# Banded attention heads in tiles of 64 queries of two heads by 128 keys, a quarter of the tokens for four heads in each turn

## The reference

```python
def swa_sink_attention(q, k, v, sinks):      # q: [B,S,8,64], k, v: [B,S,2,64]
    ...
    kb, vb = band(kc), band(vc)              # keys: the chunk before and the own one, 128 in all
    s = jnp.einsum('bnqhgd,bnkhd->bnhgqk', qc, kb).astype(jnp.float32) * scale
    s = s - slopes[None, None, :, :, None, None] * dist[None, :, None, None, :, :]
    s = jnp.where((k_pos >= 0)[None, :, None, None, None, :], s, NEG)
    ...
    m = jnp.maximum(jnp.max(s, axis=-1, keepdims=True), sink)
    p = jnp.exp(s - m)
    denom = jnp.sum(p, axis=-1, keepdims=True) + jnp.exp(sink - m)
    out = jnp.einsum('bnhgqk,bnkhd->bnqhgd', (p / denom).astype(v.dtype), vb)

def forgetting_attention(q, k, v, f_logit):  # 8 heads, block of 128 queries against all keys
    ...
    s = s + c_i[..., None] - c_keys[:, :, None, :]
    s = jnp.where(k_pos[None, :] <= q_pos[:, None], s, NEG)
    p = jax.nn.softmax(s, axis=-1).astype(v.dtype)
```

## Time and profile before

| | |
|---|---|
| median of 3 runs | 2611.76 us (2611.57 to 2616.79) |
| the profiled execution | 2613.85 us, span of its instructions 2612.2 us |
| TensorE busy, matmuls | 2429.0 us (93%), 11856 |
| TensorE weight loads busy | 2010.5 us (77%) |
| DVE busy | 1412.0 us (54%) |
| ScalarE busy | 1189.6 us (46%) |
| DMA packets | 196858, 436.30 MB |

### The profile page before, as it was taken

How to read it: one execution, slowest core, us unless ns; L and a number is a source line. 1 busy time by engine, 2 the same in 40 slices (tenths; PEclk the granted TensorE clock), 3 DMA queues, 4 the chain that set the end, 5 groups by cost and what they waited for, 6 DMA issues and landing times.

```text
span 2612.2 us, 35075 instructions
## 1 busy us (share of the span) xinstructions
PE 2429.0 (93%) x11856; PEld 2010.5 (77%) x11856; DVE 1412.0 (54%) x2376; ACT 1189.6 (46%) x2257; POOL 759.7 (29%) x623
## 2 busy tenths in 40 slices
PE   7999999599999999599889999899999999999978
PEld 6788887488888888388668887688888788888856
DVE  6311111388888788456574446744456665444464
ACT  6211111487888788322255555455553233233232
POOL 2000000011111111123355666765653532100471
PEclk9999999699999999799999999899999999999999
DMA  5333333866766664677545443465447865454563
GB/s 170 121 120 120 121 121 129 192 155 162 175 169 150 160 155 114 172 226 233 176 150 162 148 148 119 133 202 157 142 147 289 298 208 177 146 173 153 206 245 137
DMA packets 196858, 436.30 MB, mean 167 GB/s; under 512 B 19432, under 2 KB 81640, under 8 KB 183144
## 3 DMA queue, kind: packets, MB, share of 16 engines
q1 hardware_dynamic: 190576, 417.86, 51.3%
q0 software_dynamic: 6144, 16.79, 2.7%
HBM read 298.06 MB, written 136.51 MB: 166 GB/s over the span
## 4 chain that ended last, share of the span: by engine, by line
PE 41%; DVE 4%; POOL 3%; DMA 1%; issue 1%; ACT 0%; SPq 0%; ACTq 0%; DVEq 0%
PE f_ps L1901 21%; PE f_ps L1922 19%; POOL h_raw L1618 2%; DVE f_hop_lo L1804 2%; DVE f_op_lo L1793 1%; DMA h_raw<-in_w_down 1%; POOL f_b_late L1618 1%; DVE f_acc L1835 0%; DVE f_op_lo L1796 0%; DMA f_b_late<-in_w_down 0%; DVE f_u L1823 0%; DVE hop_lo L1809 0%; DVE hop_lo L1815 0%; ACT f_hop_hi L1702 0%; DVE f_hop_lo L1815 0%
## 5 line engine op out<-in xcount | busy, mean ns | idle before, releaser
L1901 PE MATMUL f_ps<-f_hop_hi,f_op_hi 128*128 128x512 f32 x768 | 305.3, 398 | 26.6 <-DVE f_u L1823 16.1
L650 POOL DMA_DIRECT2D o_main<-a_o x64 | 40.6, 635 | 926.8 <-ACT a_o L970 820.5
L1901 PE MATMUL f_ps<-f_hop_lo,f_op_hi 128*128 128x512 f32 x768 | 303.9, 396 | 0.0
L1901 PE MATMUL f_ps<-f_hop_hi,f_op_lo 128*128 128x512 f32 x768 | 303.9, 396 | 0.0
L1793 DVE TENSOR_TENSOR f_op_lo<-wu_raw,f_op_hi 128x512 fp32r<-128x512 f32 x160 | 167.1, 1046 | 222.7 <-ACT f_op_hi L1669 222.7
L874 DVE TENSOR_TENSOR a_pt_lo<-a_ps_t,a_pt_hi 128x512 fp32r<-128x512 f32 (+3 forms) x384 | 234.7, 618 | 95.2 <-ACT a_pt_hi L963 92.7
L1796 DVE TENSOR_TENSOR f_op_lo<-h_raw,f_op_hi 128x512 fp32r<-128x512 f32 x224 | 188.5, 844 | 163.9 <-ACT f_op_hi L1673 163.9
L1922 PE MATMUL f_ps<-f_hop_hi,f_op_hi 128*128 128x512 f32 x672 | 262.8, 391 | 12.4 <-DVE f_op_lo L1796 12.4
L1922 PE MATMUL f_ps<-f_hop_lo,f_op_hi 128*128 128x512 f32 x672 | 261.6, 389 | 0.0
L1922 PE MATMUL f_ps<-f_hop_hi,f_op_lo 128*128 128x512 f32 x672 | 261.5, 389 | 0.0
L963 ACT ACTIVATE a_pt_hi<-a_ps_t 128x512 fp32r<-128x512 f32 (+3 forms) x384 | 204.1, 541 | 108.1 <-PE a_ps_t L763 62.7
(11 more groups left out here) (173 smaller groups left out, 5644.9 us busy)
## 6 DMA issues: line engine op xcount, KB each, us to landing
h_raw<-u_ops SPq DMA_DIRECT2D x224, 256.0 KB, 3.8
wu_raw<-in_w_up SPq DMA_DIRECT2D x32, 1024.0 KB, 7.1
u_ops<-f_u SPq DMA_DIRECT2D x128, 256.0 KB, 4.8
u_ops<-f_us SPq DMA_DIRECT2D x96, 256.0 KB, 2.0
proj_hi<-p_o_hi SPq DMA_DIRECT2D x18, 1024.0 KB, 4.0
proj_lo<-p_o_lo SPq DMA_DIRECT2D x18, 1024.0 KB, 6.7
h_raw<-in_w_down SPq DMA_DIRECT2D x32, 512.0 KB, 4.2
h_raw<-in_w_down SPq DMA_DIRECT2D x49, 256.0 KB, 4.1
```

The source lines that it names most:

```text
L1901: last = nc.tensor.matmul(bank[:], w[:, k], h[i][:, k], start=(UP_OPENS[i] and k == 0 and m == 0), stop=(k == 3 and m == 2), skip_group_ch ...
```

## The change

- **Tiles.** A band tile is now 64 queries of two heads (128 rows) by 128 keys, exactly the band of one chunk of 64. Each turn works on a quarter of the tokens (`SPAN` = 512) for the four heads that share a key/value head, not on all tokens for one head. A turn has 16 such tiles as before, in five chunks of 4, 4, 4, 2 and 2 tiles, and 4 band steps instead of 8: 44 steps in all. Each band step is an output block of its own. There are 8 value tiles, in two groups.
- **Order.** Fox block 0's chunks move from steps 0 to 2 of their turn to steps 36 to 41 of the turn before. Block 1's stand at 0 to 4 (before 2 to 7), block 2's at 5 to 11 (8 to 14), block 3's at 12 to 23 (16 to 27), the next band chunks at 26 to 30 (30 to 37). Counted in fox steps, blocks 2 and 3 stay where they were within a step.
- **Loads.** The band loads of a turn become 19 DMAs instead of 10, with half the bytes: queries 64 x 8 x 64 in pieces of 256 bytes, keys and values 64 x 576. `proj_hi` and `proj_lo` get 64 columns of zeros in front. The fox loads keep sizes and number, but go in another order. The band's reciprocals are stored by four DMAs instead of one.

```diff
+PAD = CHUNK
...
+            for dst in (proj_hi, proj_lo):
+                for row in (P + SWA_HEADS * HEAD_DIM, P + (SWA_HEADS + SWA_KV_HEADS) * HEAD_DIM):
+                    sp.dma_start(dst[row:row + P, 0:PAD], zeros[:]).then_inc(pad_stored, 16)
...
-    steps = [("swa", j) for j in range(QT // 2)] + [("fox", b, k) for b in range(QB) for k in range(4 * b + 4)]
+    QUARTERS = SWA_HEADS // SWA_KV_HEADS
+    WINDOWS = S // CHUNK // QUARTERS
+    SPAN = WINDOWS * CHUNK
+    NSW = WINDOWS // 2
+    steps = [("swa", j) for j in range(NSW)] + [("fox", b, k) for b in range(QB) for k in range(4 * b + 4)]
...
-    swa_chunks = [("swa", j) for j in range(QT // 2)]
+    swa_chunks = [("swa", n) for n in range(5)]
+    swa_tiles = [range(0, 4), range(4, 8), range(8, 12), range(12, 14), range(14, 16)]
     chunk_at = [[] for _ in range(NSTEP)]
-    for b, (start, span) in enumerate(((0, 3), (2, 6), (8, 7), (16, 12))):
+    for b, (start, span) in ((1, (0, 5)), (2, (5, 7)), (3, (12, 12))):
         for n, c in enumerate(fox_chunks[b]):
             chunk_at[start + n * span // len(fox_chunks[b])].append(c)
     for n, c in enumerate(swa_chunks):
-        chunk_at[30 + n * 9 // len(swa_chunks)].append(("next",) + c)
+        chunk_at[26 + n * 6 // len(swa_chunks)].append(("next",) + c)
+    for n, c in enumerate(fox_chunks[0]):
+        chunk_at[36 + n * 6 // len(fox_chunks[0])].append(("next",) + c)
     turn_at = [[] for _ in range(NSTEP)]
     for g in range(4):
-        turn_at[2 + g].append(("v", "fox", g))
-        turn_at[42 + g].append(("v", "swa", g))
-    turn_at[38].append(("r",))
+        turn_at[g].append(("v", "fox", g))
+    for g in range(2):
+        turn_at[38 + 2 * g].append(("v", "swa", g))
+    turn_at[34].append(("r",))
...
             def load_fox(h):
-                load_qk("fox", QF + h * DH, KF + h * DH, qk_loaded["fox"])
+                all_cols = slice(PAD, PAD + S)
+                load_halves(q_fox.bitcast(F32), QF + h * DH, all_cols, qk_loaded["fox"])
+                load_k("fox", KF + h * DH, all_cols, qk_loaded["fox"])
                 load(decay_sb[:], decay[bass.ds(h, 1)].rearrange("a s -> (a s)").partition_broadcast(P),
                      qk_loaded["fox"])
...
-                    sp.wait_ge(scored, chunk_count(h, ("swa", QT // 2 - 1)))
-                    sp.wait_ge(v_done["swa"], 4 * (h + 1))
-                    sp.wait_ge(sink_exped, h + 1)
+                    sp.wait_ge(sink_exped, 2 * (h + 1))
                     load_swa(h + 1)
                 if not last:
                     sp.wait_ge(scored, chunk_count(h, ("fox", 3, 3, 3)))
-                    sp.wait_ge(v_done["fox"], 4 * (h + 1))
                     load_fox(h + 1)
...
+                    for n, m in enumerate(swa_tiles[what[1]]):
+                        w, pair = divmod(m, 2)
+                        for p, kk in enumerate((k_hi, k_lo)):
+                            last = nc.tensor.matmul(ps_s[ring][:, n * P:(n + 1) * P],
+                                                    q_swa[:, pair, w],
+                                                    kk["swa"][:, w * CHUNK:w * CHUNK + P],
+                                                    start=(p == 0), stop=(p == 1))
...
                     if (b, t, n) == (0, 0, 0):
-                        pe.wait_ge(qk_loaded["fox"], h * 112 + 112)
+                        pe.wait_ge(qk_loaded["fox"], QK_FOX * (head + 1))
...
-                    for m, (k, c0, c1, o0, o1) in enumerate(parts):
+                    for half in range(2):
+                        cols = slice(half * GROUP * CHUNK, (half + 1) * GROUP * CHUNK)
                         for pt in (hi, lo):
+                            last = nc.tensor.matmul(bank[:, cols], v_st[kind][:, 2 * step[1] + half], pt[:, cols],
+                                                    start=(pt is hi), stop=(pt is lo), skip_group_check=True)
...
-                    if i == 36:
+                    if i == 27:
                         invert_fox(h)
```

More of the change, by code:

```diff
@@ new lines, in load_k, with load_swa @@
+            def load_k(kind, rows, cols, done):
+                for dst, src in ((k_hi, proj_hi), (k_lo, proj_lo)):
+                    for part in range(2):
+                        load(dst[kind][part * DH:(part + 1) * DH].bitcast(F32), src[bass.ds(P + rows, DH), cols], done)
+            def load_swa(h):
+                kv, done = h // GROUP, qk_loaded["swa"]
+                at = h % GROUP * SPAN
+                load(alibi[:], alibi_dram[bass.ds(h, 1)].rearrange("a p v n c -> (a p) v n c"), done)
+                for part, half in ((0, proj_hi), (1, proj_lo)):
+                    for g in range(GROUP):
+                        load(q_swa[part * DH:(part + 1) * DH, g // 2, :,
+                                   g % 2 * CHUNK:(g % 2 + 1) * CHUNK].bitcast(F32),
+                             half[bass.ds(P + (kv * GROUP + g) * DH, DH), bass.ds(PAD + at, SPAN)].rearrange(
+                                 "d (w s) -> d w s", s=CHUNK), done)
+                load_k("swa", KA + kv * DH, bass.ds(PAD + at - CHUNK, CHUNK + SPAN), done)
+                for n in range(2):
+                    for i in range(2):
+                        load(sink[i * DH:(i + 1) * DH, n:n + 1],
+                             sinks[0, bass.ds(kv * GROUP + 2 * n + i, 1)].partition_broadcast(DH), done)
+                load_halves(v_t["swa"], VA + kv * DH, bass.ds(PAD + at - CHUNK, CHUNK + SPAN), v_loaded["swa"])
@@ new lines, in score @@
+                if what[0] == "swa":
+                    if what[1] == 0:
+                        dve.wait_ge(qk_loaded["swa"], QK_SWA * (head + 1))
+                        nc.vector.tensor_scalar(sink_neg[:], sink[:], -1.0, None, ALU.mult).then_inc(sink_negated, 1)
+                        dve.wait_ge(sink_negated, head + 1)
+                        if h is not BEFORE:
+                            dve.wait_ge(turned, turn_count(h, ("p", NSW - 1)))
+                            dve.wait_ge(sink_exped, 2 * head)
+                    nc.vector.nop(nofuse=True)
+                    for n, m in enumerate(swa_tiles[what[1]]):
+                        w, pair = divmod(m, 2)
+                        at = swa_stat(m)
+                        last = nc.vector.tensor_tensor_reduce(
+                            out=swa_cols(m), in0=ps_s[ring][:, n * P:(n + 1) * P],
+                            in1=alibi[:, 0 if w == 0 else 1, pair], scale=-SCALE, scalar=sink_neg[:, pair:pair + 1],
+                            op0=ALU.add, op1=ALU.min, accum_out=neg_max["swa"][:, at:at + 1])
+                else:
+                    _, b, t, n = what
+                    if (b, t, n) == (0, 0, 0):
+                        dve.wait_ge(qk_loaded["fox"], QK_FOX * (head + 1))
+                    if (t, n) == (0, 0) and h is not BEFORE:
+                        if b == 0:
+                            dve.wait_ge(turned, turn_count(h, ("p", BLOCK0[1] - 1)))
+                        else:
+                            dve.wait_ge(turned, turn_count(h - 1, ("p", NSTEP - 1)))
@@ L896, in _ @@
                 dve.sem_inc(done, 1)
-            for c in swa_chunks:
-                score(BEFORE, ("next",) + c)
+            for c in pre_chunks[:len(swa_chunks)]:
+                score(BEFORE, c)
             dve.wait_ge(const_in, 32)
@@ L903, in _ @@
                 copy_out(BEFORE, g)
+            for c in pre_chunks[len(swa_chunks):]:
+                score(BEFORE, c)
             def turn(h, last=False):
@@ L1010, in tables @@
     causal = np.where(k > q, NEG, 0.0).astype(np.float32)
-    k = np.arange(2 * P)[None, :] - P
-    band = (k // CHUNK <= q // CHUNK) & (k // CHUNK >= q // CHUNK - 1)
+    dist = np.abs(np.arange(P)[:, None] % CHUNK - (np.arange(P)[None, :] - CHUNK))
     slopes = 2.0 ** (-8.0 * np.arange(1, SWA_HEADS + 1) / SWA_HEADS)
-    alibi = np.where(band, -slopes[:, None, None] * np.abs(q - k) / scale, NEG).astype(np.float32)
+    group = SWA_HEADS // SWA_KV_HEADS
+    alibi = np.zeros((SWA_HEADS, P, 2, 2, P), np.float32)
+    for h in range(SWA_HEADS):
+        for pair in range(2):
+            rows = h // group * group + 2 * pair + np.arange(P) // CHUNK
+            alibi[h, :, :, pair] = (-slopes[rows][:, None] * dist / scale).astype(np.float32)[:, None]
+        if h % group == 0:
+            alibi[h, :, 0, :, :CHUNK] = NEG
     return causal, alibi
```

285 lines of the change are left out of this document (131 added, 154 removed).

## The result

The changed kernel takes 2633.85 us (median of 4 runs, 2631.09 to 2636.84), the kernel before 2611.84 (2611.57 to 2616.79): 1.0074 times as long, 95% interval 1.0062 to 1.0086. It is slower by some 20 us, where no change was forecast and the range ended at 2630. The profiled execution took 2631.09 us, with a span of 2629.4 against 2612.2.

The account below looks back on a forecast made before the run. TensorE was taken to lead the attention stage thinly, so all engines were priced; -44 - 5.6 + 40.6 + 13.3 - 6.5 + 2.4 = +0.2 us on 2611.8 gave 2612 us, range 2588 to 2630.

Parts of the forecast that it names:

- part 1: TensorE's band scores, band steps and value transposes in the attention stage: 5.5 us less a turn, -44 us in eight turns.
- part 4: Granted clock at half for 5 us behind each load wait: 1.9 us in each of seven turns, +13.3 us.
- part 3: TensorE waits 5.8 us for the next head's fox loads at fox block 0's first chunk, seven turns: +40.6 us.
- part 2: DVE and ScalarE work shrinks too; where band chunks are scored 0.8 us a turn gained, seven turns: -5.6 us.
- part 6: Dense first steps 0 to 4 of a turn: fox block 1's transposes come later, 0.3 us x 8, +2.4 us.
- Part 5: Load-bound start of the attention stage: fewer load microseconds ahead of the first fox chunk, -6.5 us (-9 to -3).
- Rival 1: Fox loads alternating between partition halves overlap, so load wait and clock fall vanish: 2558 us; chance 0.06.
- Rival 2: Fox loads overlap in part, 3 us less wait a turn, or the clock does not fall: 2591 to 2599; chance 0.20.
- Rival 3: ScalarE's output copies at a turn's fifth block wait for stores, 8 x 3 us: 2636; chance 0.20 together with Rival 4.
- Rival 4: Clock costs its full 3.4 us or dense steps lose 1 us more: 2620 to 2623; chance 0.20 with Rival 3.

Follow-up runs that it names:

- experiment 8: Changed kernel with each fox head's query, key and decay loads cut, columns 0 to 511 first, no chunk moved: 2597.49 us, ratio 0.9932.
- experiment 10: Experiment 9's kernel with fox block 2's chunks at steps 5 to 12 and block 3's at 13 to 24: 2605.18 us, ratio 0.9968.
- experiment 7: Kernel before with its loop over heads written out on every engine: 2607.44 us, ratio 0.9965.
- experiment 2: Kernel before, old tiles kept, with fox block 0 scored in the turn before at steps 40, 40-odd to 44: 2666.09 us, ratio 1.0187.
- experiment 5: Changed kernel with fox block 0 at steps 40, 40, 41 and 42 and the loop over heads written out: 2585.49 us, ratio 0.9881.
- experiment 6: Changed kernel, loop kept, with fox block 0 at steps 40 to 42 and fox block 1 at steps 1 to 4: 2589.19 us, ratio 0.9899.
- experiment 3: Changed kernel with its loop over heads written out on every engine: 2626.98 us, ratio 1.0046.
- experiment 9: Changed kernel with fox block 0 at steps 40 to 42, loop written out and columns 0 to 511 of fox loads first: 2587.21 us, ratio 0.9899.

## Why the prediction was wrong

All of it per turn, from the two windows over five turns and the seven turns from the first head to the last:

| term | forecast | measured | from |
|---|---|---|---|
| TensorE's work (part 1) | -5.5 | -5.3 | TensorE busy 342.1 us in five turns, 315.4 in experiment 8 (one clock fall in each) |
| the clock (part 4) | +1.9 | +1.4 | TensorE busy 322.4 in five turns, 315.4 in experiment 8 |
| load wait (part 3) | +5.8 | +4.4 | 30.5 us in seven turns |
| other idle time (parts 2 and 6) | -0.5 | +3.3 | idle 10.5 less 4.0, against 3.3 |
| sum | +1.7 | +3.7 | 26.2 us in seven turns (the terms give 3.8) |

**Parts 2 and 6: the step that failed.** The prediction let DVE and ScalarE, with less work, keep in step with TensorE: where band chunks are scored 0.8 us a turn were to be gained (part 2, -5.6 us), and at the dense first steps "in step with each other they lose what they lost before, about 1 us" (part 6, +2.4 us in all). TensorE's idle time apart from the load wait grew by 3.3 us a turn instead, 23 us in seven turns, which is more than the whole difference between the kernels. By place in a turn it is this:
- At the band chunks 1.2 us, where a gain was forecast. ScalarE's work in the turn fell by 4.3 us, nearly the forecast 4.4 (busy 289.2 to 267.7 in five turns), but a mean over the turn hides that chunks of four tiles put four exponentials in front of one copy. With the new tiles this idle time stands in every run, with the loop and without, with the load wait and without (2.45 to 2.50 us; 2.0 where a clock fall lies in the stretch; only experiment 10, with block 3 later, differs). With the old tiles it does not, in the old order (experiment 7, 1.33) nor in the new one (experiment 2, 1.32). So the tiles did it. That the four exponentials are the reason is read from ScalarE's timeline; no run tried smaller chunks of the same tiles.
- At the start of a turn, from the last fox weighing to the first of the next, 1.9 us (0.7 to 2.6). Some 1.2 of them are the jump back, which the prediction did not price: without it the idle time here falls from 2.6 to 0.7 us in the changed kernel and from 0.7 to 0 in the kernel before (experiments 5 and 7). The other 0.7 are waits for output copies: experiment 5, without a jump, has 4.6 us of them in seven turns. Each band step is now an output block of its own.
- In the first ten fox steps 0.5 us (0.2 to 0.7). Experiment 10 was to tell why and could not; it stays open.
- The rest of the turn gives back 0.3.

**Part 1, TensorE's work: right.** In the loops the difference is 5.3 us a turn (against experiment 8) or 5.5 (experiment 6), with both kernels written out (experiments 5 and 7) 5.0; 5.5 was forecast. Band score matmuls stand 0.11 us apart, and the four weighing matmuls of a band step 0.12, as priced.

**Part 3, the load wait: mechanism right, too large by a quarter.** The landing was right: 20.3 to 20.9 us after the first issue behind the first turn, 20.2 forecast. TensorE's arrival was not. The row that it started from was right, 15.4 us in six of the seven turns before (16.9 in the one with the clock fall). But less work in bands (parts 1 and 2) was to bring TensorE forward by 1.0 us to 14.4, and it came at 16.7 in all seven turns, since the steps with band chunks in front of it had become longer. So this error is the failed step once more, seen from the other side: what TensorE loses at the band chunks it need not wait at the loads. That the two errors partly cancel was luck.

**Part 4, the clock: somewhat too large.** The fall is 3.4 us and not 5, and cost 1.4 us a turn and not 1.9. The relief from hidden waits is 0.3 us (half of 3.4, less 1.4), not 0.6.

**Part 5, the start: near.** The first fox chunk came at 494.50, "near 494", 5.8 us earlier than before, where 6.5 was forecast for the start. With one turn's saving of 5.2 the forecast comes to 11.7 us outside the seven turns, and 8.1 at the start and 0.9 at the end came: as in the turns, the idle time took part of the saving.

**The rivals.** Rival 1 (the loads overlap) is refuted by the two query loads 2.5 us apart. The prediction read the table of ports in the Trainium skill as speaking for the overlap. The same page of the Trainium skill (SBUF — State Buffer, "Can I just issue two DMAs to hit both halves?") says that two transfers at once, one into a tile at partition 0 and one at partition 64, gave only 6% more than a single one and ran one behind the other. The trace agrees. Rival 2 (partial overlap, or no fall of the clock) did not happen: the load wait was shorter since TensorE came later, not since the loads came sooner. Rival 3 (ScalarE waits for output stores) did not happen: no wait of ScalarE's for a store is in the trace, only TensorE's short waits for ScalarE's copies. Its 2636 lies next to the measured time by chance. Rival 4 (2620 to 2623) had one half of the reason, the dense steps, but gave them 1 us; its other half, the full price of the clock, did not come.

## What to carry to other kernels

A change that takes work off the leading engine and gives a transfer a deadline should be priced at the deadline first: here 30 us of waiting and some 10 us of half clock stood, in seven turns, against 37 us of saved work, and moving four chunks by two to four steps, one line, turned 0.7% slower into 0.6% faster. Savings ahead of such a wait are worth little until it is gone (the written-out turns gained 7 us with it and 15 without), and two cures for one wait don't add up. Where all engines are nearly as busy as the first (DVE and ScalarE had 85% of TensorE's busy time in the kernel before), price the stretches and not the turn: how many units of the second engine's work stand between two results that the first one waits for. Of the 5.0 us a turn that left TensorE, 3.0 came back as waits even without the jump (experiments 5 and 7: idle 2.5 and 5.6 us a turn), 1 of them as a rest of the load wait.

## What the runs showed of the hardware

- The jump back of a loop costs an engine more than a row shows. DVE issues nothing for 2.4 us behind it (2.37 at 729.24), and the start of a turn is 1.4 us longer with the jump than without in one kernel and 2.3 in the other. The Trainium skill (Advanced Engine Details and Errata, "Control Flow Timing") gives a compare-and-branch about 108 ns; the pause here is some twenty times that. What the engine waits for in it no run here shows.
- The length of TensorE's wait does not settle how long the clock falls behind it. Behind waits of 3.6 to 4.2 us it stayed at half for 3.4 us, behind 5.2 us on average mostly for 6.8 (experiment 3), behind 4.5 us on average for 6.8 (experiment 2). Yet in experiment 10 it fell for 10.2 us behind a wait of 1.43 us, and in the kernel before for 3.4 us behind waits of no more than 0.6.
- Loads cut into a first quarter and a rest delivered the quarter 7.7 to 8.4 us after the first issue, and the rest after 21.7 to 25.3 us (experiment 8), where the uncut loads took 20.3 to 20.9 (23.3 in the first turn). The transfer queued last, the values, was late by that (1.2 us a turn in experiment 9).
- Two loads of 512 KB from one queue land 2.5 us apart, whether both go to the same 64 partitions or one to each half.
